# The two large mixers of a fused transformer stack: gates and branch products laid out by token, and the short convolution's work moved behind four half gates

## The reference, cut to what matters

```python
h = rmsnorm(x, attn_norm_g[l])
(cq, ckv, krope, cb, cc, cx, dq, dk, dv, iq, ik, iw,
 gq, gk, gv, glr, gr, gate_pre) = jnp.split(h @ w_in[l], split_points, axis=-1)
o_mla  = mla_branch(cq, ckv, krope, ...)         # latent attention, 256 wide
o_conv = shortconv_branch(cb, cc, cx, conv_w[l]) # cb * (3-tap causal convolution of cc * cx)
o_dsa  = dsa_branch(dq, dk, dv, iq, ik, iw)      # attention over the 64 best-scored keys
o_gla  = gla_branch(gq, gk, gv, glr, gr, ...)    # gated linear attention
gates  = jax.nn.sigmoid(gate_pre).reshape(b, s, 4, d)          # 4 x 1024 columns
merged = sum over n of gates[:, :, n] * (branches[n] @ w_branch[l, n])   # 256 -> 1024 each
x = x + merged @ w_out[l]
```

## Time and profile before

| | us |
|---|---|
| median of 3 runs (lowest, highest) | 1886.12 (1885.27, 1888.9) |
| the profiled execution's own time | 1887.27 |
| its span | 1885.4 |
| first large mixer, from the `cv` tiles to the end of `down` | 1022.7 to 1235.8 |
| second large mixer, the same part | 1474.6 to 1687.8 |

### The profile page before, as it was taken

The page is one execution under the profiler, slowest core; times in us unless marked ns, Lnnn a source line. Parts: engine busy times, 40 slices in busy tenths (PEclk is TensorE's granted clock), DMA queues, the critical chain, the costliest instruction groups (busy, mean ns, idle before and its releaser), DMA issues.

```text
span 1885.4 us, 26904 instructions
## 1 busy us (share of the span) xinstructions
PE 1824.2 (97%) x10634; PEld 1582.8 (84%) x10634; DVE 1301.5 (69%) x2001; ACT 945.9 (50%) x1360; POOL 30.2 (2%) x35
## 2 busy tenths in 40 slices
PE   8999999999999999999999899899999989999998
PEld 7888877888888887888888789888888889978886
DVE  6774785776587656677656877777745877677763
ACT  5554655554455445555445345455535444455552
POOL 0000000000000001000000000000000000000000
PEclk9999998999999998999999999999999999999999
DMA  7666513656566654366655433565565433456652
GB/s 245 191 178 196 169 58 99 190 169 203 176 182 186 202 183 136 96 194 172 208 165 163 138 112 118 164 195 182 183 197 165 133 105 113 148 186 191 186 186 97
DMA packets 248054, 309.37 MB, mean 164 GB/s; under 512 B 22574, under 2 KB 217294, under 8 KB 247930
## 3 DMA queue, kind: packets, MB, share of 16 engines
q1 hardware_dynamic: 247622, 306.57, 52.8%
q10 hardware_dynamic: 308, 1.09, 0.1%
HBM read 306.57 MB, written 1.05 MB: 163 GB/s over the span
## 4 chain that ended last, share of the span: by engine, by line
PE 76%; issue 11%; DVE 8%; ACT 3%; DMA 1%; SPq 0%; DVEq 0%; POOLq 0%; POOL 0%; ACTq 0%
PE ps L636 20%; PE ps L588 13%; PE ps L589 12%; PE ps L590 12%; PE ps L637 10%; DVE wlo L1605 3%; ACT whi L1169 1%; PE ps L834 1%; PE ps L797 1%; PE ps L771 1%; PE ps L1077 1%; DVE m_scr L2177 1%; PE ps L741 1%; PE ps L784 1%; DVE m_scr L1614 1%
## 5 line engine op out<-in xcount | busy, mean ns | idle before, releaser
L1605 DVE TENSOR_TENSOR wlo<-staging,whi 128x1024 fp32r<-128x1024 f32 (+2 forms) x598 | 698.1, 1183 | 399.6 <-ACT whi L1169 399.0
L1169 ACT ACTIVATE whi<-staging 128x1024 fp32r<-128x1024 f32 (+2 forms) x598 | 606.3, 1025 | 459.3 <-PE ps L590 258.5
L636 PE MATMUL ps<-hT,whi 128*128 128x512 f32 x1984 | 699.6, 397 | 3.0 <-DVE hT L1614 3.0
L637 PE MATMUL ps<-hT,wlo 128*128 128x256 f32 x1984 | 557.5, 281 | 0.0
L636 PEld LDWEIGHTS ps<-hT,whi 128*128 128x128 f32 x1984 | 373.1, 188 | 92.9 <-DVE hT L1614 4.2
L637 PEld LDWEIGHTS ps<-hT,wlo 128*128 128x128 f32 x1984 | 375.9, 189 | 0.0
L588 PE MATMUL ps<-hT,whi 128*128 128x256 f32 x800 | 234.1, 293 | 23.4 <-DVE wlo L1605 23.4
L590 PE MATMUL ps<-hT,wlo 128*128 128x256 f32 x800 | 228.6, 286 | 0.0
L589 PE MATMUL ps<-hT,whi 128*128 128x256 f32 x800 | 228.5, 286 | 0.0
L588 PE MATMUL ps<-whi,fh 128*128 128x512 f32 (+1 forms) x528 | 209.5, 397 | 0.0
L589 PE MATMUL ps<-wlo,fh 128*128 128x512 f32 (+1 forms) x528 | 209.5, 397 | 0.0
(11 more groups left out here) (323 smaller groups left out, 1985.3 us busy)
## 6 DMA issues: line engine op xcount, KB each, us to landing
staging<-in_w_in SPq DMA_DIRECT2D x92, 512.0 KB, 3.5
staging<-in_ffn_w_down SPq DMA_DIRECT2D x88, 512.0 KB, 4.1
staging<-in_ffn_w_gate SPq DMA_DIRECT2D x84, 512.0 KB, 4.5
staging<-in_ffn_w_up SPq DMA_DIRECT2D x84, 512.0 KB, 4.5
staging<-in_w_ffn_gate SPq DMA_DIRECT2D x44, 512.0 KB, 4.1
staging<-in_w_ffn_up SPq DMA_DIRECT2D x44, 512.0 KB, 4.6
staging<-in_w_ffn_down SPq DMA_DIRECT2D x44, 512.0 KB, 3.9
staging<-in_od_w_in SPq DMA_DIRECT2D x16, 512.0 KB, 3.6
```

The lines of the kernel that those rows point to most:

```text
L636: e.matmul(o, wh[:, kk, sl], hT[:, k, :], start=k == 0, stop=False)
L637: m = e.matmul(o[:, 0:256], wl[:, kk, sl], hTh[:, k, :], start=False, stop=k == KD - 1)
L1169: e.activation(whi[u % NH][:, 0:n], stage[u % NS][:, 0:n], ACT.Copy).then_inc(*K.inc("hi", ("hi", u)))
L1605: e.tensor_tensor(wlo[u % NH][:, 0:n], stage[u % NS][:, 0:n], whi[u % NH][:, 0:n].bitcast(F32), ALU.subtract).then_inc(*K.inc("lo", ("lo", ...
```

## The change

1. The sixteen gate quarters become eight halves by token (`x_cols`, 512 columns): 48 matmuls of 512 columns each, two banks. DVE's multiplication by R goes; ACT takes the tanh straight from PSUM with half the norm factor as its scale (new `st8[:, 6:8]`).
2. The sixteen merge quarters become eight halves: 12 matmuls of 512 columns, the branch stationary, two banks. A merge unit now has 1024 columns in place of 512, so a mixer has 69 units, and had 77. DVE works on 1024 elements at once.
3. The merged sum is now by token, and `down` needs it by feature: a new generator `turn()` transposes it (16 transposes in 4 banks), ACT and DVE read high and low part from PSUM.
4. The `cv` tiles come behind the four halves of gates 1 and 3 (rounds 25 to 30), `short_conv` starts in round 30 and not 14, with its taps spread over two rounds; on ACT the high part of y comes in round 34. The merges of branch 1 follow in rounds 35 and 36. The order of the other merges changes from 1, 3, 2, 0 to 1, 2, 3, 0.
5. `mla()` waits two rounds fewer ahead of its attention; `down` is part of `gates()` and is woven with the rest; `mla_load` on SP no longer waits for branch 1; GpSimd's loops, which split nothing, are gone.

```diff
-FILL = _fill()
-BEFORE = {3: 1, 2: 3, 0: 2}
+FILL = [("gate", 1, 0), ("gate", 1, 1), ("gate", 3, 0), ("gate", 3, 1), ("cv", 0, 0), ("cv", 1, 0), ("cv", 2, 0),
+        ("gate", 2, 0), ("merge", 1, 0), ("merge", 1, 1), ("gate", 2, 1), ("merge", 2, 0), ("gate", 0, 0), ("merge", 2, 1), ("merge", 3, 0),
+        ("merge", 3, 1), ("merge", 0, 0), ("gate", 0, 1), ("merge", 0, 1)]
+BEFORE = {2: 1, 3: 2, 0: 3}
+TURN = 52, 57
...
 # TensorE
-                            two_tiles = tiles_in_turn(g, room((P, "gate", q)), (P, "gate mm", q))
...
+                            yield from x_cols(g, 2648 + 1024 * n + 512 * h, 512)
...
+                        wh, wl = view(w[0], (2, 512)), view(w[1], (2, 512))
+                        if h == 0:
+                            e.wait_ge(*K.at(P, "branch", n))
+                        users = [(P, "merge", n, h, t) for t in range(2)]
+                        ps = room_pair(*users)
+                        for t in range(2):
+                            sl = slice(128 * t, 128 * t + 128)
+                            for k in range(2):
+                                mm = three(ps[t], m.bh[:, 2 * n + k, sl], m.bl[:, 2 * n + k, sl], wh[:, k, :], wl[:, k, :],
+                                           k == 0, k == 1)
...
+                    yield from down(g, m.rows)
+
+                def turn():
...
+                        for q in (2 * h, 2 * h + 1):
+                            ps = room((P, "turn", q))
+                            e.wait_ge(*K.at(P, "acc", 0, h))
                             for j in range(2):
+                                for t in range(2):
+                                    c, k = (2 * j + t) * 128, 2 * q + j
+                                    w = e.transpose(ps[:, c:c + 128], m.G[:, 1, t, 128 * k:128 * k + 128], ident)
...
 # ACT
+                        yield from x_cols(512)
+                        if (n, h) == (2, 0):
+                            e.wait_ge(*K.at(P, "branch", 1))
+                        if (n, h) == (0, 0):
+                            e.wait_ge(*K.at(P, "kn mm", 1))
+                        for t in range(2):
+                            user = ("in", g, 2648 + 1024 * n + 512 * h, t)
+                            e.wait_ge(*K.at("in mm", *user[1:]))
+                            e.activation(m.G[:, n, t, 512 * h:512 * h + 512], bk(*user), ACT.Tanh,
+                                         scale=st8[:, 6 + t:7 + t]).then_inc(
...
 # DVE
-                            e.tensor_tensor(G[:, 2 * q:2 * q + 2, :], two(bk(P, "gate", q)), R22, ALU.mult).then_inc(
...
+                        stt(gg, gg, 1.0, PS[:, b:b + 2, :], ALU.add, ALU.mult).then_inc(*K.inc("merge", *steps))
+                        if n != 1:
+                            e.wait_ge(*K.now("merge"))
+                            e.wait_ge(*K.at(P, "acc", BEFORE[n], h))
+                            e.tensor_tensor(o, o, gg, ALU.add).then_inc(*K.inc("merge", (P, "acc", n, h)))
...
-                weave([(1, gates()), (14, short_conv()), (1, dsa()), (5, gla()), (27, mla())], catch_up)
-                weave([(1, down(g, m.rows, 1.0))], catch_up)
+                weave([(1, gates()), (30, short_conv()), (1, dsa()), (5, gla()), (27, mla()), (TURN[0], turn())], catch_up)
```

More of the change, by code:

```diff
@@ L330, in build @@
         ev, od = A["ev_w_in"][0], A["od_w_in"][0]
-        first, pooled = [], set()
+        first = []
         def plan_ffn(i):
@@ L1129, in mla @@
                         done(P, "kn", t)
-                    for _ in range(7):
+                    for _ in range(5):
                         yield
@@ L1439, in gates @@
                     yield from project(X2[2:4])
-                    for q in range(3):
-                        yield
-                        side.due += 2
-                        yield
-                    for kind, *what in FILL:
-                        if kind == "gate":
-                            q = 4 * what[0] + what[1]
+                    e.wait_ge(*K.at("half", g))
+                    for kind, n, h in FILL:
+                        if kind == "cv":
                             yield
@@ new lines, in gates, with turn @@
+                    yield from down(m.rows)
+                def turn():
+                    for h in range(2):
+                        if h:
+                            for _ in range(TURN[1] - TURN[0]):
+                                yield
+                        for q in (2 * h, 2 * h + 1):
+                            b = m.place[q]
+                            e.wait_ge(*K.at(P, "turn mm", q))
+                            e.wait_ge(*K.at(P, "merge mm", b // 2, 1))
+                            e.activation(flat(m.bh[:, b:b + 2, :]), bk(P, "turn", q), ACT.Copy, scale=0.5).then_inc(
+                                *K.inc("merge_hi", (P, "high", q)))
@@ new lines, in gates, with turn @@
+                        yield
+                    yield from down(g, m.rows, 1.0)
+                def turn():
+                    for h in range(2):
+                        if h:
+                            for _ in range(TURN[1] - TURN[0]):
+                                yield
+                        for q in (2 * h, 2 * h + 1):
+                            b = m.place[q]
+                            e.wait_ge(*K.at(P, "high", q))
+                            stt(flat(m.bl[:, b:b + 2, :]), bk(P, "turn", q), 0.5, flat(m.bh[:, b:b + 2, :]).bitcast(F32),
+                                ALU.mult, ALU.subtract).then_inc(
+                                *K.inc("merge_lo", (P, "low", q), ("ev", (P, "turn", q))))
```

279 lines of the change are left out of this document (74 added, 205 removed).

## The result

| | before | after |
|---|---|---|
| median, four runs each (lowest, highest) | 1887.23 (1885.27, 1888.9) | 1854.62 (1853.28, 1858.81) |
| ratio, 95% interval | | 0.9831 (0.9812 to 0.9851) |
| profiled execution's own time | 1887.27 | 1854.08 |
| its span | 1885.4 | 1852.3 |
| first large mixer, first `cv` or gate matmul to the end of `down` | 213.1 | 198.1 |

The change is faster by 1.7%: 32.6 us, where 26.6 were forecast.

What follows compares the result with a forecast made beforehand. TensorE's matmuls were taken as the bound wherever it is fed, DVE in the top-k rounds. The terms summed to -13.3 us a mixer, -26.6 for two, from 1887.27 to 1860.7, as a median 1860; range 1843 to 1879.

Steps and rivals of the forecast that it cites:

- Part 1: Gates by token: 384 matmuls of 512 columns for 768 of 256, 87.2 us for 92.2, a gain of 5.0 a mixer.
- Rival (e): Gates run at `down`'s pace with its waits, 0.236 us a matmul, gaining 1.6 and not 5.0: 1866 us; chance 0.10.
- It is on no path of its own: DVE's multiplications by R, 11.0 us a mixer, fall away; their worth is only in DVE's load.
- Part 2: Merges by token gain 0.6 us a mixer; the sixteen added transposes (turns) lose 1.8.
- Part 3: Short convolution leaves the top-k rounds, where DVE is the bound: 6.0 us a mixer taken, bounds 3 to 9.
- Part 4: Tail, the last merges and gates: of 7.0 us of waits and slow clock, 5.5 taken as gain, bounds 2 to 7.
- The cause is in the sizes: Tail's waits: a merge unit lasts TensorE 1.44 us but needs 2.06 of DVE; after, 2.8 against 3.6.
- Part 5: New waits a mixer: 1.5 us for branch 1 at its first merge, 0.5 for a bank handed on within one step.
- rival (c): Branch 1 late, TensorE stands 6 us at the first merge, old waits kept: 1894 us, slower; chance 0.06.
- Rival (a): DVE stays the bound; only 3 us come back in the top-k rounds and 3 in the tail: 1871; chance 0.22.
- Rival (b): All waits go, also the small ones of the `cv` tiles and `down`: 1845 us; chance 0.08.

Runs made afterwards that it cites:

- e7: Changed kernel with sixteen idle DVE operations of 128 x 512 a mixer where the multiplications by R stood: a mixer 3.6 and 4.2 us longer.
- e1: Changed kernel with the `cv` tiles ahead of the gates again and the short convolution starting in round 14: 1874.57 us.
- e2: Kernel before, with eight DVE operations of the short convolution (4.1 us a mixer) left out, so its result is wrong: a mixer 5.3 and 5.1 us shorter.
- e11: Kernel before, with branch 0's four gates directly behind branch 3's merges, then all eight merges of branches 2 and 0: total that of the kernel before.
- e3: Changed kernel with merges by token in quarters (12 matmuls of 256 columns): at equal clock a mixer at most 0.6 us longer than the changed kernel.
- e8: Changed kernel, but a gate half gives its four units back in pairs: ratio to the kernel before 0.9841, against 0.9837 for the changed kernel.
- e9: Changed kernel with both merges in quarters and gate units given back in pairs: ratio to the kernel before 0.9861.
- e6: Changed kernel with GLA from round 6, not 5, and branch 1's merges behind both halves of gate 2: 1843.74 us.
- e10: Kernel before, with branch 2's two pairs of merges that shared a step each put in steps of their own: ratio 0.9991.
- e5: Changed kernel with the second half of gate 2 ahead of branch 1's merges: 3.6 us faster by the medians, intervals overlapping.

## Why the prediction was right, and where not

The mixer fell by 15.0 us (213.1 to 198.1); the sum said 13.3. Point by point, in its order:

- **Part 1, gates: right, the size a little high.** 332 of the 384 matmuls run undisturbed, 0.2285 us apart in the mean, where the undisturbed ones by feature had 0.1197; at their own pace that is 87.7 us for 91.9: 4.2 and not 5.0. With seams (the places where a gate's matmuls meet another branch's step), slow clock and waits they take 94.4 (0.246). Rival (e)'s reason, the side work between the steps, holds at the seams, but the old layout has as many of them. The Trainium skill's rule in "TensorE: Matmul & The Clock Gate", section "Back-to-back issue gap", by which, as an estimate, 1.0 us of it would have been left, doesn't hold here at either size (0.120 and 0.230 us measured). "It is on no path of its own" was right as put; e7 prices what was counted in the load.
- **Part 2: right.** Merges and `down` together run at 0.2354 a matmul, 45.2 us for 192 of them; the turns take 1.6 us for the 1.8 forecast, and nothing waits behind them.
- **Part 3: right in mechanism, low in size.** The 5.84 us wait and its 1.4 us of low clock are gone in full. 6.0 was taken; e1 gives 8.8 to 10.4 for undoing it, above the upper bound of 9 in one mixer, more than half of that low clock; e2 gives 4.0 of waits for half of the work. In the second mixer before, the low clock behind the same 5.84 us cost 2.5.
- **Part 4: right in place, and its reason doesn't carry to the new kernel.** All 7.0 us went (5.5 taken), and 1.4 of them were low clock. In the second mixer before, the same wait of 2.03 is followed by full pace, and the tail is 5.6 us over its work: 5.5 was the right size for the waits. "The cause is in the sizes" holds for the old layout: e11 shows the debt, 1.92 us of DVE against 1.44, in one piece. But small units in the new layout (e3) bring no wait back. What differs is that DVE no longer multiplies by R, each gate half lasts TensorE 11 us, in which DVE catches up, and units come free singly; e8 and e9 make the last of these a part of it, 1.2 us. How the rest divides stays open: the R multiplication was not put back on the chain from a gate's end to its tanh.
- **Part 5: the step that failed.** "For a bank that is handed on within one step ... I add 0.5": the place and the two instructions were named, the price was not. The wait was 1.44 in both mixers, since ACT's copy stood behind two tanh. The low clock behind it cost 1.7 more in the first mixer, 3.1 for 0.5, and nothing in the second. Branch 1's wait was 1.05 for 1.5 taken: rival (c)'s step was there, far from the 6 us it needed.

With these sizes the sum of the first mixer reads -4.2 - 0.4 (merges) + 1.6 - 7.4 (top-k) - 7.0 + 1.1 + 3.1 = -13.2, and `down`, which lost 1.0 us of small waits, makes it -14.2 of the measured -15.0. That the forecast came so near is luck in part: two errors met, 2.9 us too little for the old waits, 2.6 too little for the new one. 1.4 us of the first and 1.7 of the second are low clock, which came in one mixer and not in the other. The second mixer gained 1.4 us more than the first, which the prediction held to be alike; the matmuls and the new wait are the same there, but after has no low clock in it.

Rival (a), DVE as the bound, was wrong though its load was right: DVE is busy 42.5 of 46.8 us in the top-k rounds and TensorE hardly waits. e7 shows how near it was: 11 us more of DVE, and 3.9 us come back. Rival (b) named what e6 reaches by two edits in the order of rounds: 1844 against its 1845.

## What to carry to other kernels

When a layout change doubles what a step holds (two banks for one, two tanh for one), look at every bank that is emptied and refilled within one step, and put a step between: here one number in the table of start rounds was worth 3.5 to 6.5 us a mixer. Price a new wait as a range, from its length alone to its length with low clock behind it: the same wait cost 1.4, 3.1 or 4.9 us here. Before two profiles are compared to a microsecond, compare the time that each spent at the lower clock. A debt of one engine was moved and not paid by reordering (e10, e11); less work for it, or longer work of the other engine between, is what the changed kernel has, though which of them removed the tail's waits is not shown.

## What the runs showed of the hardware

- A wait of 1.4 us can bring TensorE's clock to its lower level, and need not. The wait of L1080 for ACT (1.39 to 1.46 us) is on record eight times, in both mixers of after, of its second run, of e3 and of e5. Low clock followed it five times (in after's first mixer twelve matmuls of 512 columns took 4.42 us, most of the first eight 0.42 to 0.43 apart and not 0.23), full pace three times. In the two mixers of after TensorE did the same matmuls in the same order ahead of it.
- It is so with longer waits too: behind 2.03 us in the tail of the kernel before, the clock fell in the first mixer (0.21 us apart, from 0.8 us behind the wait) and not in the second (0.12). Behind the wait of 1.05 us at 1132.59 the matmuls start 0.23 apart, the full pace. The first matmul behind a wait doesn't tell: in e2 it shows 0.36, and the low clock comes 0.9 us later.
- A matmul next to another branch's step costs about 0.1 us more than one in a stream, at both sizes: 0.30 to 0.35 us for 0.23 by token, 0.19 to 0.23 for 0.12 by feature, about 30 times among the gates of the first mixer in both layouts. Fewer and longer matmuls didn't thin out these seams.
